# The second layer's output projection as three products of fp32r halves, with its weight chunks ahead of its modulation chunks

## The reference, cut to what matters

```python
h = rms_norm(x, norm1_g[1])
mix, q_mem = mla_mixer(h, positions, b_w_in[0], ...)        # z = h @ b_w_in, 1344 columns
mem_out = memory_attention(q_mem, mem_k, mem_v, ...)
x = x + jnp.concatenate([mix, mem_out], axis=-1) @ b_w_out[0]   # (256 x 1536) @ (1536 x 1024)
x = x + hierarchical_moe(rms_norm(x, norm2_g[1]), ...)       # 32 experts, weights of 3 MB each
```

## Time and profile before

| | us |
|---|---|
| median of 3 runs | 1541.68 (1540.25 to 1543.96) |
| the profiled execution, its own time | 1530.78 |
| its span, first to last instruction | 1529.0 |
| output projection of the second layer, first matmul to last add | 527.6 to 571.8 |
| second mixture of experts, to the next stage's first matmul | 572.1 to 809.9 |
| its first expert product (L1666) | 590.1 |
| kv projection: its weights issued, w_ada 7 given back, first product | 435.0, 441.9, 474.6 |

### The profile page before, as it was taken

One profiled execution on the slowest core, in us unless ns is written; L12 is line 12 of the kernel. 1 busy time (PEld: TensorE's weight loads), 2 busy tenths in 40 slices (PEclk: granted clock), 3 DMA queues, 4 the chain that ended last, 5 costly groups with the idle time before them and its releaser, 6 DMA issues. The chain is left out here.

```text
span 1529.0 us, 23552 instructions
## 1 busy us (share of the span) xinstructions
PE 1421.7 (93%) x9090; PEld 775.5 (51%) x9090; DVE 735.2 (48%) x1655; ACT 493.4 (32%) x980; POOL 103.6 (7%) x258
## 2 busy tenths in 40 slices
PE   8999999978899899998888998899899998989998
PEld 4485533322375644332226886788655336755432
DVE  1468332222255535222226755675585346668534
ACT  3232211111226403111116655665613116661211
POOL 0000011100000001111102000200001102000110
PEclk9999999999999999999999999999999999999999
DMA  8798799999973197999998452236169996438996
GB/s 357 296 360 339 320 367 421 420 421 421 426 304 129 48 398 317 383 422 421 420 424 347 166 198 106 111 138 233 44 239 421 420 423 248 183 148 324 422 420 283
DMA packets 63400, 469.80 MB, mean 307 GB/s; under 512 B 7809, under 2 KB 15921, under 8 KB 18738
## 3 DMA queue, kind: packets, MB, share of 16 engines
q1 hardware_dynamic: 63282, 468.22, 75.6%
HBM read 465.42 MB, written 2.76 MB: 306 GB/s over the span
## 5 line engine op out<-in xcount | busy, mean ns | idle before, releaser
L1666 PE MATMUL PS<-ring,catT 128*32 128x512 f32 x3072 | 348.0, 594 | 16.0 <-issue 16.0
L821 PE MATMUL PS<-w_split,h_split 128*128 128x512 f32 x1152 | 269.9, 393 | 6.1 <-DVE w_split L906 6.1
L821 PEld LDWEIGHTS PS<-w_split,h_split 128*128 128x128 f32 x1152 | 213.5, 188 | 56.2 <-DVE w_split L906 8.5
L1666 PEld LDWEIGHTS PS<-ring,catT 128*32 128x32 f32 x3072 | 96.1, 110 | 232.5 <-issue 232.2
L906 DVE TENSOR_TENSOR w_split<-ring,w_split 128x512 fp32r<-128x512 f32 x192 | 133.6, 711 | 66.3 <-ACT w_split L854 65.9
L1689 PE MATMUL PS<-ring,row_place 128*32 128x512 f32 x1232 | 143.9, 600 | 22.9 <-issue 22.9
L854 ACT CAST w_split<-ring 128x512 fp32r<-128x512 f32 x192 | 118.0, 619 | 103.9 <-PE PS L821 103.5
L1866 ACT ACTIVATE row_place<-PS 128x256 f32<-128x256 f32 x48 | 18.4, 384 | 364.9 <-PE PS L1666 364.9
L1689 PEld LDWEIGHTS PS<-ring,row_place 128*32 128x32 f32 x1232 | 41.9, 110 | 115.9 <-issue 115.6
L507 PE MATMUL PS<-ring,catT 128*128 128x512 f32 x224 | 97.0, 593 | 2.6 <-DMA ring<-in_b_w_out 1.6
L1559 POOL COPY catT<-xsT 128x256 f32 x176 | 63.3, 404 | 405.7 <-PE PS L1666 398.2
(11 more groups left out here) (440 smaller groups left out, 1861.7 us busy)
## 6 DMA issues: line engine op xcount, KB each, us to landing
ring<-in_moe SPq DMA_DIRECT2D x269, 1024.0 KB, 15.4
ring<-in_w_ada SPq DMA_DIRECT2D x16, 3072.0 KB, 12.6
ring<-in_a_w_in SPq DMA_DIRECT2D x23, 2048.0 KB, 14.2
ring<-in_b_w_in SPq DMA_DIRECT2D x8, 2048.0 KB, 20.9
first_down<-in_moe SPq DMA_DIRECT2D x8, 1024.0 KB, 8.2
ring<-in_a_w_out SPq DMA_DIRECT2D x2, 3072.0 KB, 17.7
ring<-in_b_w_out SPq DMA_DIRECT2D x2, 3072.0 KB, 13.9
ring<-in_w_mem_kv SPq DMA_DIRECT2D x2, 2048.0 KB, 11.5
```

What stands on the lines that cost most here:

```text
L821: last = nc.tensor.matmul(PS[:, 2 * (i % 2) + t, :], hs[:, hp, k, t * P:(t + 1) * P], wk[:, (KT * i + k) % splits, wp, :], start=k == 0 an ...
L1666: last = nc.tensor.matmul(PS[lanes, 4 + i % 2, :].rearrange("p (g f) -> p g f", g=2), xf[:, i % 2, k, lanes], gate_up_weights(2 * i + q % ...
```

## The change

Two things change. The output projection of the second layer is no longer `project_rows` but a new `project_out_split`: ACT and DVE split each of the 24 weight slices into two fp32r halves, three buffers deep (`wk`), ACT and POOL split the 12 slices of `catT` (`hs`), and PE does 6 matmuls for each slice (3 products x 2 token tiles) in fp32r. The 12 modulation columns are placed singly among the DVE's subtractions: one behind every second slice of c = 0, one behind each of the slices 3 to 8 of c = 1. The two chunks that c = 0 uses (w_ada 8 and the first weight chunk) are given back together at its end, those of c = 1 at its end.

Second, the chunk order: before, a w_ada chunk lies ahead of each of the first two weight chunks in both projections. Now the input projection's is weight, w_ada, weight, w_ada, weight, and the output projection's is w_ada, weight, weight, w_ada.

```diff
@@ -196,10 +196,10 @@
         c_ain = weight_amid("a_w_in", 8, [512] * 5, [0, 1, 0, 1, 1])
         c_aout = weight_amid("a_w_out", 12, [512] * 2, [2, 1])
         c_moe0 = experts("moe0", 32, ASIDE[0])
-        c_bin = weight_amid("b_w_in", 8, [512, 320, 512], [1, 1, 0])
+        c_bin = weight_amid("b_w_in", 8, [512, 320, 512], [0, 1, 1])
         c_qup = weight("b_w_q_up", 4, [1536])
         c_kvup = weight("b_w_kv_up", 2, [2048])
-        c_bout = weight_amid("b_w_out", 12, [512] * 2, [1, 1])
+        c_bout = weight_amid("b_w_out", 12, [512] * 2, [1, 0], 1)
         c_moe1 = experts("moe1", 32, ASIDE[1])
         c_ain2 = weight("a_w_in_2", 8, [512] * 18)
         c_aout2 = weight_amid("a_w_out_2", 8, [512] * 2, [1, 0], 2)
@@ -553,7 +553,7 @@
                             for _ in range(ada[c]):
                                 ada_part(dve, ada0 + done, silu_row)
                                 done += 1
-                            if ada_last:
+                            if c + ada_last >= len(widths):
                                 ada_part(dve, ada0 + done, silu_row, False)
                                 done += 1
                             if done == n_ada and after is not None:
@@ -576,6 +576,100 @@
...
+        def project_out_split(first):
+
+            K, SPLITS = 12, 3
+            with ExitStack() as ctx_rows:
+                silu_row, *early_homes[1] = early_places(ctx_rows, 1)
+                hs = sbuf(ctx_rows, "h_split", [P, 2, K, T], F32R)
+                wk = sbuf(ctx_rows, "w_split", [P, SPLITS, 2, BANK], F32R)
+                h_high, h_low = sig("ph_source_high"), sig("ph_source_low")
+                w_high, w_low, w_used = sig("ph_weight_high"), sig("ph_weight_low"), sig("ph_weight_used")
+                out_chunk = (first + 1, first + 2)
+                block = ctx_rows.enter_context(nc.Block())
+
+                @block.sync
+                def _(sp):
+                    load_silu_row(silu_row)
+                    wr, br = router_weights(1)
+                    nc.sync.dma_start(wr, A["wr1"]).then_inc(r_loaded.sem, 16)
+                    nc.sync.dma_start(br, A["br1"].partition_broadcast(P)).then_inc(r_loaded.sem, 16)
+                    stream.issue(nc, sp, first)
+                    load_early_down(1, (0, 1))
+                    load_early_more(1)
+                    stream.issue(nc, sp, out_chunk[1])
+
+                @block.gpsimd
+                def _(pool):
+                    for j in range(K):
+                        pool.wait_ge(*h_high.at(j + 1))
+                        nc.gpsimd.tensor_tensor(hs[:, 1, j, :], catT[:, j, :], hs[:, 0, j, :].bitcast(F32), ALU.subtract).then_inc(h_low.sem, 1)
+
+                @block.tensor
+                def _(pe):
+                    for c in range(2):
+                        for j in range(K):
+                            if c == 0:
+                                pe.wait_ge(*h_low.at(j + 1))
+                            pe.wait_ge(*w_low.at(K * c + j + 1))
+                            for t in range(TT):
+                                for n, (hp, wp) in enumerate(((0, 0), (0, 1), (1, 0))):
+                                    last = nc.tensor.matmul(PS[:, 2 * c + t, :], hs[:, hp, j, t * P:(t + 1) * P], wk[:, (K * c + j) % SPLITS, wp, :],
+                                                            start=j == 0 and n == 0, stop=j == K - 1 and n == 2)
+                            last.then_inc(w_used.sem, 1)
+                    keep_busy(4, 2)
+
+                @block.scalar
+                def _(act):
+                    nc.scalar.activation(stat[:, 2, 30:31], ones_f[:, 0:1], ACT.Sqrt)
+                    for c in range(2):
+                        act.wait_ge(*stream.landed(out_chunk[c]))
+                        w = stream.view(out_chunk[c], K)
+                        for j in range(K):
+                            i = K * c + j
+                            if c == 0:
+                                nc.scalar.copy(hs[:, 0, j, :], catT[:, j, :]).then_inc(h_high.sem, 1)
+                            if i >= SPLITS:
+                                act.wait_ge(*w_used.at(i - SPLITS + 1))
+                            nc.scalar.copy(wk[:, i % SPLITS, 0, :], w[:, j, :]).then_inc(w_high.sem, 1)
+
+                @block.vector
+                def _(dve):
+                    def add(c, t):
+                        dve.wait_ge(*w_used.at(K * (c + 1)))
+                        r = x[:, t, c * BANK:(c + 1) * BANK]
+                        nc.vector.tensor_tensor(r, r, PS[:, 2 * c + t, :], ALU.add)
+
+                    def ada_column(c, n):
+                        if n == 0:
+                            dve.wait_ge(*stream.landed(ada_at[c]))
+                        w = stream.view(ada_at[c], 6)
+                        return nc.vector.tensor_tensor_reduce(w[:, n, :], w[:, n, :], silu_row, 1.0, 0.0, ALU.mult, ALU.add, ada_out[:, 6 * c + n:6 * c + n + 1])
+
+                    dve.wait_ge(*silu_loaded.at(16))
+                    for c in range(2):
+                        dve.wait_ge(*stream.landed(out_chunk[c]))
+                        w = stream.view(out_chunk[c], K)
+                        for j in range(K):
+                            i = K * c + j
+                            dve.wait_ge(*w_high.at(i + 1))
+                            nc.vector.tensor_tensor(wk[:, i % SPLITS, 1, :], w[:, j, :], wk[:, i % SPLITS, 0, :].bitcast(F32), ALU.subtract).then_inc(w_low.sem, 1)
+                            if c == 0 and j % 2 == 1:
+                                last = ada_column(8, j // 2)
+                            elif c == 1 and j in (1, 2):
+                                add(0, j - 1)
+                            elif c == 1 and 3 <= j < 9:
+                                last = ada_column(9, j - 3)
+                        dlink(last)
+                        dve.wait_ge(*w_low.at(K * (c + 1)))
+                        nc.vector.sem_inc(chunk_used, 2)
+                    modulation(0, (0, 48), (0, 1))
+                    add(1, 0)
+                    add(1, 1)
...
@@ -2736,7 +2830,7 @@
                     k_squared, stat_ready, roots_ready = sig("ph_source_high"), sig("ph_weight_low"), sig("ph_source_low")
                     q_roped, k_normed = sig("ph_normed"), sig("ph_weight_high")
                     unit_ready, taken_act, taken_dve = sig("rows_ready"), sig("ph_taken_act"), sig("ph_taken_dve")
-                    z_chunk, q_chunk, kv_chunk = (c_bin + 1, c_bin + 3), c_qup, c_kvup
+                    z_chunk, q_chunk, kv_chunk = (c_bin, c_bin + 2), c_qup, c_kvup
 
                     Z, ZT, Q, KV, QN, QR, KN, KR = 0, 4, 7, 13, 21, 25, 27, 31
                     by_act = [n < ZT or Q <= n < KV or n >= KV and n % 2 == 1 for n in range(33)]
@@ -2971,8 +3065,9 @@
                         dlink(nc.vector.tensor_scalar(stat[:, 1, 2:2 + TT], stat[:, 1, 0:TT], EPS, None, ALU.mult))
                         dve.wait_ge(*silu_loaded.at(16))
                         for c in range(2):
-                            ada_part(dve, 6 + c, silu_row)
+                            ada_part(dve, 6 + c, silu_row, False)
                             dve.wait_ge(*unit_ready.at(2 * c + 2))
+                            used()
                             used()
                         for which in range(2):
                             for i, (half, part_of) in enumerate(((0, 0), (1, 1), (0, 1), (1, 0))):
@@ -3048,7 +3143,7 @@
                             "v": lambda kt: vv[:, kt, h, :],
                             "out": catT[:, h:h + 2, :].rearrange("p h t -> p (h t)") if h % 2 == 0 else None}
                 attention([mla_head(h) for h in range(8)], True, row_scale=qs[:, 2])
-            project_rows(catT, 12, c_bout, [512] * 2, add_rows(None), ada=[1, 1], after=lambda: modulation(0, (0, 48), (0, 1)), router=1)
+            project_out_split(c_bout)
         if stop >= 4:
             moe(1, c_moe1, 32, col("norm2_g", 8, 8), None, None, "norm")
         first_block.close()
```

3 lines of the change are left out of this document (added).

## The result

The changed kernel took 1549.12 us in the median of 11 runs (1540.75 to 1558.80), the kernel before 1540.10 us of 11 (1532.21 to 1543.96) measured with it: a ratio of 1.0072, 95% interval 1.0052 to 1.0092, so 9 us slower by the medians and 11 by the ratio, where 5.3 were forecast. The profiled execution of the changed kernel took 1549.63 us, its span was 1547.9 us, and its mean granted clock 0.971 (0.984 in the profile of before). Run once more on another chip it gave 1.0082 (1.0052 to 1.0112).

A forecast was written before the change was run, and what follows sets the result against it. PE bounds moe1 first, then the weight stream; both were forecast to shift alike. The wait for w_ada 9 turns a paper gain of 5.5 us into +5.3, so 1541.7 + 5.3 = 1547.0 us, range 1541.5 to 1551.0.

The forecast's parts named there:

- The input order: Input projection: its new chunk order is worth 0, at most 0.7 us; later kv weights stay hidden under the q projections.
- rival B: Output projection: w_ada 9 lands in 11.4 us or later and PE's clock falls in the second pause; +7 to +10, chance 0.12.
- Part 2, t0: Output projection: DVE's c = 0 takes 18.8 us and gives its chunks back at t0 = 550.4, bounds 547.2 and 551.3.
- POOL's price: In c = 0, nine POOL subtractions hold DVE up by 0.53 us each, 2.4 to 4.8 in sum; 3.9 taken.
- PE's cold clock in the first half: After PE's pause until 532.4, a clock of 0.50 costs 1.5 us of PE work, hidden by DVE's slower pace.
- Part 3, the landing: w_ada 9 leaves at 550.5 on an empty queue and lands 10.0 us later; stage ends at 577.1 against 571.8, +5.3 us.
- Part 4, the stream: Weight stream around the output projection: 18.1 us of free DMA time against 12.7, +5.4 us, so the shift passes whole.
- a moe1 whose length differs from before by over 1 us: Sign that would show part 4 wrong: the second mixture's length was to stay within 1 us of before.
- The cap on what a quicker stage brings: Free stream time up to t0 of 10.3 us against 12.7 limits a quicker stage's gain to 2.4 us.
- rival C: Output projection faster, as w_ada 9 isn't waited for: stage -4.2 us, or -2.4 if the stream caps it, 1539.3; chance 0.10.
- The reading of the stream as a second clock: In moe1 the weight stream paces beside PE; an earlier microsecond reaches the end only if the stream is also further on.
- the sum: Whole kernel: the shift of 5.3 us carries unchanged into the median, 1541.7 + 5.3 = 1547.0 us, +0.34%.

The follow-up runs named there:

- input_order: The kernel before with only the input projection's chunk order changed to weight, w_ada, weight, w_ada, weight: 1538.7 us, ratio 0.9998 to before.
- four_ahead: The changed kernel with the kv up projection's chunk ahead of the query's, so all four output projection chunks are loaded before the stage: 1542.1 us, ratio 1.0026 to before.
- fast_stage: The changed kernel with zeros for w_ada 9's columns and GpSimd's low halves, 12 constant matmuls at PE's start, a later silu wait: 1532.7 us, ratio 0.9961 to before.
- fillers: The changed kernel with 20 constant matmuls before PE's first slice and 26 before slice 4 of c = 1: 1543.2 us, ratio 1.0022 to before.
- after: The changed kernel itself, with both parts of the change, against the kernel before: 1549.1 us, ratio 1.0072.
- after_again: The changed kernel once more, unchanged, on another chip: 1549.0 us, ratio 1.0082 to before.
- output_only: The changed kernel with the input projection's chunk order put back as before: 1550.6 us, ratio 1.0085 to before.
- pool_memset: The changed kernel with GpSimd writing zeros, reading nothing, in place of the activations' low halves: 1542.4 us, ratio 1.0030 to before.
- again: The kernel before once more, unchanged, as a second profile of it: 1541.2 us, ratio 1.0011 to before.

## Why the prediction was right and wrong

**Right.** The mechanism, its place and its sign: w_ada 9 issued at 551.87 (forecast 550.5), DVE idle on it 6.97 us (5 to 6), PE's longest pause before slice 4 of c = 1, slices 1.75 apart (1.85), full DMA share from the stage's end on, the first expert product at 597.56 (595.5). The input order was worth 0, shown by `input_order`. 1549.1 lies in the range, but the loss is twice the forecast's by the ratio, and its size is rival B's (+7 to +10): as B had it, the landing took over 10 us and the clock fell in the second pause.

**Part 2, t0.** Forecast 550.4, measured 551.8: +1.4. Two terms were too small. The first is POOL's price: the 4.8 "if a column is held up as a subtraction is" was discounted to 3.9 us, but four columns of 1.76 beside POOL and three pairs of subtractions of 1.82 to 2.35 instead of 1.28 make it 4.4. By the Trainium skill (SBUF — State Buffer, section "Who interferes with whom") the columns had to pay as well, and with the rule t0 would have been 551.3. The trace agrees with it in the columns of 1.76. The second is PE's cold clock in the first half, which DVE's slower pace was to hide: DVE waited 1.3 us in sum for ACT and so for PE, and where constant matmuls went ahead of the first slice, w_ada 9 went out 0.5 and 0.9 us sooner.

**Part 3, the landing.** Forecast 10.0 us "with the queue empty", measured 11.0 (10.9 to 11.2 in all eleven profiles that load it there): +1.0. Six pieces went out right behind it each time; that they slow it is argued, not shown. Against it: in `four_ahead` a chunk of 3 MB took 10.1 with another of 3 MB sent 0.4 us behind it. From the landing to the last addition it took 16.3 us, forecast 16.6. Sum 5.3 + 1.4 + 1.0 - 0.3 = 7.4, the measured shift.

**Part 4, the stream.** Free DMA time rose by 6.4 us (19.1 against 12.7; forecast 5.4), beside a last addition that comes 7.4 later. From the last addition to its own end moe1 took 231.5 us against 233.0, so the sign "a moe1 whose length differs from before by over 1 us" did show; but two profiles of the kernel before differ in it by 2.4 (233.0 and 230.6), and so it says nothing. The cap on what a quicker stage brings (rival C, and the 3 us that `fast_stage` was expected to gain) was too low, since it counted free time alone. In `fast_stage` that fell by 4.3 us (7.7 against 12.0 in the first 73 us), but the bytes moved rose by 8 us' worth: with the DMA share near 1 the rate still differed, 375 GB/s in one window of before (620.6 to 640.6, share 0.97) and 411 in the same of `fast_stage` (share 1.01). The reading of the stream as a second clock itself isn't refuted: over the 17 profiles moe1's end goes with the bytes moved in the first 150 us by 2.5 us per MB, with a scatter of 0.9 us (w_ada 9 added where it was sent ahead), and with the last addition with a scatter of 1.5.

**The step that failed** is the sum: "a wait for data and DVE work should be the same number of microseconds" in the median, with the cold clock of the first pause put at nothing ("which DVE's slower pace hides") and that of the second met only in rival B. Of the 9 us in the medians, or 11 by the ratio (11 to 13 in the three kernels with this stage), the stage's terms give 7.4; the other 4 to 6 by the ratios have no term in the sum. What the runs show in its place: they hang, at least in part, on what PE does in its two pauses. With constant matmuls in both, the stage ends only 0.25 us sooner, but the ratio falls from 1.0072 to 1.0022.

The clock is the likely link, and it is argued. The mean clock of all runs of the changed projection with both pauses cold (after, after_again, output_only: 27 runs) is 0.973, that of before's runs 0.980; from run to run of one kernel, 0.001 of clock goes with 1.03 us (the slope over all timed runs, each kernel's mean taken out). That slope doesn't say which causes which. Where the two cold stretches of 6.8 us are filled, clock and excess are gone, and more than the excess: 1.0022 is 3.4 us (0.5 to 6.5), with a last addition 7.1 us later than before's.

A rough plane through the 16 ratios gives 0.8 us for each us of the stage's length and 0.35 us for each us at 1.2 GHz in the 58 us from the stage's start (14.1 us in the changed kernel, 3.4 before), with a constant of 0.6 and a scatter of 2 us; the 0.35 is known to some 0.13. For the changed kernel that is 7.4 x 0.8 + 10.7 x 0.35 + 0.6 = 10.2, where the ratio says 11. The second term is what the forecast left out. The plane is worst at `pool_memset`, which is 4.3 us quicker than it says, with both cold stretches in place: so this price is an estimate and not shown.

The Trainium skill (TensorE: Matmul & The Clock Gate, section Terms) puts the penalty of time at a reduced clock at that time, times the share of the clock that is lost. By it the two stretches of 6.8 us would cost 6.8 us, an estimate from the page's rule. What `fillers` gave back in the medians, 5.9 us, is near that, but the trace doesn't show it where the stretches lie: there the last addition moved by 0.25 us.

**Still open** is where those 4 to 6 us are. The two stretches themselves lower the mean clock by 6.8 / 1548 = 0.0044; the kernel before has one of 3.4 us behind its stage, so 0.0033 of the 0.007 observed is accounted for, and the rest must be cold time elsewhere, some 11 us. From moe1's end to the end of the program the profiles take 724 to 739 us, and it is mostly there that executions differ: that part holds 33 to 66 us at 1.2 GHz and takes 0.39 us more for each of them (correlation 0.95 over the 17 profiles). At that price 11 us would be 4.5, the size that is missing; that is an estimate. But the kernel before (before, again, input_order) has 33, 66 and 60 us of it there, the changed stage (after, after_again, output_only) 62, 47 and 37: no difference that single profiles can tell. Neither is it shown whether a stretch at the lower clock makes later ones likelier.

## What to carry to other kernels

Before reordering a ring, follow each chunk to the event that frees its place: a chunk moved to the end of a stage's order may be issued only by that stage's own midpoint, and an in-order engine that does side work on it holds all that is queued behind. Put such side work as late as it can stand (5.5 us here for moving six instructions). When PE pauses for several us, try matmuls on constants in the pause even where its slower restart seems hidden, and judge by many timed runs and not by the stage's end in one profile: here they were worth 5.9 us in the median and 0.25 in the stage, for a reason that stays open.
